# The sums of x for the seven products: copies on ScalarE and sums on VectorE instead of eight operations on GpSimd

## What is computed

```python
SUBS = ["ffn0", "mix1", "ffn"] + ["ffn", "mix1", "ffn"] + ["ffn", "mix2", "cross", "ffn"] * 2
```

```python
def swiglu(x, w_gate, w_up, w_down):
    return (jax.nn.silu(x @ w_gate) * (x @ w_up)) @ w_down
```

## Time and profile before

| | |
|---|---|
| three runs | 2532.86, 2539.4, 2545.09 us; median 2539.4 |
| the profiled execution | 2531.94 us, of which the span of its instructions 2530.2 us |
| mean granted TensorE clock | 0.984 of full speed |
| busy, of the span | TensorE 96%, VectorE 72%, ScalarE 51%, GpSimd 12% |
| GpSimd in `x_sums` | 57.0 us in L2767 and 41.6 us in the four sums, for seven sublayers |

### The profile page before, as it was taken

One profiled execution on the slowest core, in us unless ns is written; L12 is line 12 of the kernel. 1 busy time (PEld: TensorE's weight loads), 2 busy tenths in 40 slices (PEclk: granted clock), 3 DMA queues, 4 the chain that ended last, 5 costly groups with the idle time before them and its releaser, 6 DMA issues.

```text
span 2530.2 us, 30855 instructions
## 1 busy us (share of the span) xinstructions
PE 2421.6 (96%) x12522; PEld 2056.3 (81%) x12522; DVE 1834.1 (72%) x1797; ACT 1297.2 (51%) x1388; POOL 303.7 (12%) x414
## 2 busy tenths in 40 slices
PE   8999998998999998998999999989989999999898
PEld 6889986786789986886889878867877898788677
DVE  6656778868866779768757667688688667577894
ACT  5445445545537545535535664555355356644552
POOL 0100102102200121121100000111021000000210
PEclk9999999999999999998999999989999999999999
DMA  9755444854754435845864445448548544454473
GB/s 330 244 185 207 163 162 158 282 201 165 273 209 169 159 140 202 288 179 187 288 214 173 159 162 204 178 166 270 212 167 282 196 167 159 146 207 164 183 264 110
DMA packets 82549, 504.43 MB, mean 199 GB/s; under 512 B 11608, under 2 KB 12760, under 8 KB 30184
## 3 DMA queue, kind: packets, MB, share of 16 engines
q1 hardware_dynamic: 61488, 433.23, 47.4%
q0 software_dynamic: 19744, 67.65, 8.4%
q10 hardware_dynamic: 1176, 1.58, 0.4%
HBM read 476.72 MB, written 25.69 MB: 199 GB/s over the span
## 4 chain that ended last, share of the span: by engine, by line
PE 71%; DVE 15%; ACT 4%; POOL 4%; issue 4%; DMA 2%; SPq 0%; DVEq 0%; ACTq 0%; POOLq 0%
PE acc L703 17%; PE acc L705 17%; PE acc L704 17%; DVE w_lo L571 7%; PE acc L671 4%; PE acc L672 4%; PE acc L673 4%; ACT w_hi L563 3%; POOL tmp L2767 2%; DMA raw<-in_w 2%; DVE raw L2037 1%; PE aux L804 1%; PE aux L803 1%; PE aux L802 1%; PE aux L931 1%
## 5 line engine op out<-in xcount | busy, mean ns | idle before, releaser
L571 DVE TENSOR_TENSOR w_lo<-raw,w_hi 128x2048 fp32r<-128x2048 f32 (+1 forms) x459 | 1028.8, 2250 | 446.4 <-ACT w_hi L563 445.1
L563 ACT ACTIVATE w_hi<-raw 128x2048 fp32r<-128x2048 f32 (+1 forms) x459 | 860.4, 1882 | 538.4 <-PE acc L705 368.2
L703 PE MATMUL acc<-w_hi,x_hi 128*128 128x512 f32 (+1 forms) x1400 | 553.4, 395 | 43.6 <-DVE w_lo L571 40.9
L704 PE MATMUL acc<-w_hi,x_lo 128*128 128x512 f32 (+1 forms) x1400 | 546.6, 390 | 0.0
L705 PE MATMUL acc<-w_lo,x_hi 128*128 128x512 f32 (+1 forms) x1400 | 546.1, 390 | 0.0
L703 PEld LDWEIGHTS acc<-w_hi,x_hi 128*128 128x128 f32 x1400 | 266.1, 190 | 106.6 <-DVE w_lo L571 47.7
L705 PEld LDWEIGHTS acc<-w_lo,x_hi 128*128 128x128 f32 x1400 | 266.1, 190 | 55.4
L704 PEld LDWEIGHTS acc<-w_hi,x_lo 128*128 128x128 f32 x1400 | 266.4, 190 | 53.9 <-issue 1.0
L703 PE MATMUL acc<-w_hi,h_parts 128*128 128x512 f32 x704 | 274.5, 390 | 0.0
L705 PE MATMUL acc<-w_lo,h_parts 128*128 128x512 f32 x704 | 274.0, 389 | 0.0
L704 PE MATMUL acc<-w_hi,h_parts 128*128 128x512 f32 x704 | 273.9, 389 | 0.0
(11 more groups left out here) (434 smaller groups left out, 3241.8 us busy)
## 6 DMA issues: line engine op xcount, KB each, us to landing
raw<-in_w SPq DMA_DIRECT2D x399, 1024.0 KB, 4.9
squares<-tmp POOLq DMA_DIRECT2D x40, 512.0 KB, 3.7
tmp<-squares POOLq DMA_DIRECT2D x160, 128.0 KB, 4.2
raw<-in_w SPq DMA_DIRECT2D x18, 512.0 KB, 5.0
tmp<-in_norm_gb POOLq DMA_DIRECT2D x8, 1024.0 KB, 5.3
tmp<-in_norm_gb POOLq DMA_DIRECT2D x6, 512.0 KB, 3.9
tmp<-in_gate_rows POOLq DMA_DIRECT2D x12, 256.0 KB, 3.0
squares<-tmp POOLq DMA_DIRECT2D x8, 256.0 KB, 3.2
```

The lines of the kernel that those rows point to most:

```text
L563: nc.scalar.activation(w_hi[:, slot, 0:kind], raw[:, slot, 0:kind], ACT.Copy).then_inc(hi_done, 1)
L571: nc.vector.tensor_tensor(w_lo[:, slot, 0:kind], raw[:, slot, 0:kind], w_hi[:, slot, 0:kind].bitcast(F32), ALU.subtract).then_inc(lo_done, 1)
L703: nc.tensor.matmul(out, vh, wh, start=first and k == 0, stop=False)
L704: nc.tensor.matmul(out, vl, wh, start=False, stop=False)
```

## The change

In the norm ahead of an `ffn` sublayer ScalarE copies both banks of the first half, x11 and x12, as they are, to `XQ4[0]` and `XQ4[1]` (two calls of `whole`), between the square root and the `x_hi` of the second half. TensorE waits for each copy before it writes over that bank. After the first silu ScalarE copies the bank of x22 to `XQ4[2]` (a third call). VectorE makes the four sums, and takes x21 straight from its bank; they stand behind the weight sum T1, and `sum_low(0)` moves with them ahead of `times`. GpSimd no longer takes part.

```diff
@@ TensorE, x_turn
+                    if tt and N < n_subs and subs[N] == "ffn":
+                        pe.wait_ge(whole_copied, 3 * (ffns(N) - 1) + half_ + 1)
@@ ScalarE
+            def whole(N, tt, half_):
+
+                act.wait_ge(x_parts, 4 * N + 2 * tt + half_ + 1)
+                nc.scalar.activation(XQ4[2 * tt + half_ - tt], flips[half_][:, :].rearrange("p (a b) -> p a b", b=P), ACT.Copy)\
+                    .then_inc(whole_copied, 1)
@@ ScalarE, norm
                 root(N, 1)
+                if parts(N) and subs[N] == "ffn":
+                    whole(N, 0, 0)
+                    whole(N, 0, 1)
                 if parts(N):
                     x_high(N, 1)
@@ ScalarE, ups
                     silu(0, 0)
                     if s:
+                        whole(s, 1, 1)
                         sum_high(0)
@@ VectorE
+                def x_sums():
+
+                    b = f - 1
+                    x21 = flips[0][:, :].rearrange("p (a b) -> p a b", b=P)
+                    dve.wait_ge(whole_copied, 3 * b + 3)
+                    V_.tensor_tensor(XQ4[3], x21, XQ4[2], ALU.subtract).then_inc(sum_ready, 1)
+                    dve.wait_ge(sum_ready, 4 * b + 1)
+                    V_.tensor_tensor(XQ4[2], XQ4[0], x21, ALU.subtract).then_inc(sum_ready, 1)
+                    V_.tensor_tensor(XQ4[0], XQ4[3], XQ4[0], ALU.subtract).then_inc(sum_ready, 1)
+                    dve.wait_ge(sum_ready, 4 * b + 3)
+                    V_.tensor_tensor(XQ4[1], XQ4[1], XQ4[0], ALU.add).then_inc(sum_ready, 1)
@@ VectorE, ups
                         first_sum(c0 + 4)
+                    if s:
+                        x_sums()
+                        sum_low(0)
                     times(0, 0)
                     if s:
-                        sum_low(0)
                         ahead.to(c0 + 4)
                         for q in range(1, 4):
                             sum_low(q)
@@ GpSimd
-            def x_sums():
...
-                    if s:
-                        x_sums()
                     for i in range(6):
                         permute(f, i)
```

More of the change, by code:

```diff
@@ L394, in program @@
             sem(n) for n in ("silu_ready", "hid_ready", "squares_ready", "hid_hi", "hid_parts"))
-        sum_ready, sum_hi, sum_parts, kept_copied, outs_ready, kept_silu = (
-            sem(n) for n in ("sum_ready", "sum_hi", "sum_parts", "kept_copied", "outs_ready", "kept_silu"))
+        sum_ready, sum_hi, sum_parts, kept_copied, outs_ready, kept_silu, whole_copied = (
+            sem(n) for n in ("sum_ready", "sum_hi", "sum_parts", "kept_copied", "outs_ready", "kept_silu", "whole_copied"))
         squares_stored = [sem(f"squares_stored{i}") for i in range(2)]
@@ L2761, in permute @@
                     pool.dma_start(HF[i % 2][32 * b:32 * b + 32, 0:w * S].rearrange("r (a c) -> r a c", a=4), src).then_inc(hid_landed, 16)
-            def x_sums():
[L2765 to L2782, removed]
             for s in range(n_subs):
                 if is_ffn(s):
-                    f, c0 = ffns(s), base[s]
+                    f = ffns(s)
                     pool.wait_ge(x_parts, 4 * (s + 1))
```

## The result

The changed kernel takes **2480.39 us** (median of 4 runs, 2477.69 to 2482.3), the kernel before 2537.92 (median of 4). The ratio is 0.977, with a 95% interval of 0.974 to 0.980: 2.3% faster. The forecast was 2481.5 us.

A forecast was written before the change was run, and what follows sets the result against it. TensorE (96% busy) sets the time, with GpSimd's lateness behind its waits. Weight sum to chunk 5 falls from 129.25 to 71.4 us, 57.9 less: 2531.9 to 2474.0, plus 7.5 for the median gives 2481.5 us; range 2466 to 2506.

The forecast's parts named there:

- What bounds the kernel: At each ffn start: TensorE sets the time; GpSimd, 12% busy, is on the path seven times through ScalarE's order.
- The copies cost nothing: ScalarE's copies of x11, x12 and x22: hidden, costed at nothing; at most 8 us in all without that cover.
- The sums, 2.66 us: Four sums on VectorE behind the weight sum T1: 2.66 us a sublayer, bounds 2.4 and 4.4.
- upper bound: Four sums on VectorE: at most 4 x 1.10 = 4.4 us, 1.10 taken as the longest for this size.
- Chunk 5 after 10.2 us: Both engines ready to give VectorE chunk 5 10.2 us after the weight sum's start, was 18.38; seven sublayers 71.4 us.
- The same shift at GATE0, 57.9 us: GATE0 moves by the same 8.2 us in sublayer 3, VectorE then bounding the stretch; 57.9 us over all sublayers.
- The shift lasts to the end: From GATE0 through the second group to the sublayer's end everything moves together, nothing tied to another time.
- VectorE was to be 19 us busier: Expected in the changed profile: VectorE about 28 x 0.68 = 19 us more busy, GpSimd 98.6 us less.
- B: Between GATE0 and 644 something, likely a 1 MB load, gives back half the shift: 2510 us; chance 0.10.
- C: No gain: the later three sums come so late on VectorE that chunk 5 is hardly earlier: 2539 us; chance 0.03.
- E: More gain: the wait before GATE0 and its slow clock go too, another 35 us: 2447 us; chance 0.04.
- D: Slower: VectorE truly bounds the start, sums add 2.66 us a sublayer, 18.6 in all: 2558 us; chance 0.03.

The follow-up runs named there:

- Experiment 5: Kernel before, eight operations still on GpSimd; ScalarE and VectorE split chunks 5 and 6 ahead of the third and fourth sums' parts: 2521.39 us, ratio 0.993.
- experiment 3: Against the kernel before: ScalarE copies all four quarters of x, GpSimd makes the four sums, VectorE keeps its old order: 2499.3 us, ratio 0.984.
- experiment 4: Against the kernel before: GpSimd puts the four quarters together, VectorE makes the four sums from SBUF, no ScalarE copies: 2512.18 us, ratio 0.990.
- experiment 2: Changed kernel with four more dependent subtractions on VectorE ahead of the first sum of x in each of seven sublayers: 2498.35 us, ratio 0.984.
- experiment 7: Changed kernel with VectorE's low part of chunk 7 (GATE0) moved ahead of the second gate times up and the transpose: 2490.06 us, ratio 0.981.

## Why the prediction was right

*What bounds the kernel: right.* GpSimd at 12% busy was on the path, through the order of ScalarE and VectorE. Experiment 5 shows the order's part, experiments 3 and 4 GpSimd's.

*The copies cost nothing: right.* They lie in ScalarE's idle time, 3.43 us of it left.

*The sums, 2.66 us: right*, 2.65 measured. The upper bound beside it was misread: 1.10 us was not the longest that an operation of this size took, the second low part took 1.77 at 578.43 of the same trace, so the bound should have been 4 x 1.77 = 7.1 us. As GpSimd no longer runs beside the sums, it did no harm. *Chunk 5 after 10.2 us:* 10.29 to 10.42 in the seven sublayers, 72.3 us in all for 71.4.

*The same shift at GATE0, 57.9 us: right*, 57.0. That VectorE then bounds the stretch (the reason given for expecting no more) is shown by experiment 2, where 2.9 us more on VectorE became 20.4 us.

*The shift lasts to the end: right as far as the medians tell.* The profiled executions alone differ by 8 us less; the clock behind the second GATE0 makes up 6 of them, and it differs between executions of one kernel. Here luck helped the forecast: the 7.5 us added for the distance of the median from the profiled execution were not part of the mechanism, and they are about what the prediction missed for the profiled execution, which it put at 2474.0 and which took 2482.3. Between the medians this difference does not show.

*One expectation failed:* VectorE was to be 19 us busier and is not. Its added operations take that time, but the low parts of the sums and the splits of chunk 4 had been stretched while GpSimd ran: the 28 low parts took 33.9 us, 1.21 each, and take 0.69 each, 14.7 us less; the seven splits took 2.60 us and take 2.29, 2.2 us less. I read the 1.10 as a bound and did not ask what it said about the others. The same omission made the estimates for experiments 4 and 5 too low.

*The rivals.* B and C fall with the 57.5 us that were kept of 57.9 and with chunk 5 after 10.3 us; E falls with the wait before GATE0, which is 3.16 to 3.34 us in all seven sublayers. D, by which the busier engine must not be given more, is half right, and that half is experiment 2: VectorE's time is indeed the kernel's time here. But 2.65 us on VectorE removed 8 us of waiting of the same engine. The rule of the Trainium skill (Perfetto Trace Analysis, Identifying the Most-Contended Engine) ranks engines by their share over the span, and TensorE by that of its weight loads. By that measure TensorE comes first here (81%, VectorE 72%), so the rule does not by itself speak against this change; the prediction took it further than the page goes. What counted here was which engine worked last before TensorE's wait.

## What to carry to other kernels

Look at which instruction ended each repeated wait of the bounding engine and follow it back through the orders of the engines between; an almost idle engine may stand at its head. Then rebuild the stretch operation by operation with the measured spacings; here it gave the gain up to GATE0 within 2% (57.9 us for 57.0). When an order is moved, ask where the remaining wait lands: ahead of a stretch bound by another engine its slow matmuls cost little, ahead of one bound by TensorE they are paid in full (experiment 7).

## What the runs showed of the hardware that I had not expected

- Where VectorE and GpSimd ran side by side with all inputs in SBUF, one or both took longer: a VectorE sum 1.76 us for 0.68 (experiment 4), a GpSimd sum 3.21 for 1.29 (experiment 3). `times`, which has one input in a PSUM bank, took its 0.68 us at 569.56 beside GpSimd's additions.
- The same idle time of TensorE, 2.31 us, was followed by full speed at 443.90 and by the low clock at 988.61, in one execution (granted 1.00 and 0.50).
- A VectorE operation of 512 columns took 0.68 us with one input in a PSUM bank and 0.68 with both in SBUF.
